# A hybrid SSM / gated-recurrence / expert-lookup layer: two buffers instead of three and another formula in the gated recurrence

## The reference, cut to what matters

```python
def rglru_scan(x, h0, lam, w_r, b_r, w_i, b_i):
    xb = x.reshape(x.shape[0], x.shape[1], LRU_HEADS, LRU_BLOCK)
    r = sigmoid(einsum('blhi,hij->blhj', xb, w_r).reshape(x.shape) + b_r)
    i = sigmoid(einsum('blhi,hij->blhj', xb, w_i).reshape(x.shape) + b_i)
    log_a = -LRU_C * r * softplus(-lam)
    a = exp(log_a)
    bx = sqrt(-expm1(2.0 * log_a)) * (i * x)
    bx = bx.at[:, 0].add(a[:, 0] * h0)
    _, h = lax.associative_scan(linear_combine, (a, bx), axis=1)
    return h, h[:, -1]
```

## Time and profile before

| | |
|---|---|
| median of 3 executions | 2747.85 us (2744.62 to 2749.66) |
| the profiled execution, its own time | 2744.62 us |
| its span, first to last instruction | 2742.8 us |
| PE busy | 2283.4 us (83%) |
| DVE busy | 1532.9 us (56%) |
| POOL busy | 1096.0 us (40%) |
| ACT busy | 422.4 us (15%) |
| mean granted TensorE clock | 0.946 |

### The profile page before, as it was taken

The page is one execution under the profiler, slowest core; times in us unless marked ns, Lnnn a source line. Parts: engine busy times, 40 slices in busy tenths (PEclk is TensorE's granted clock), DMA queues, the critical chain, the costliest instruction groups (busy, mean ns, idle before and its releaser), DMA issues.

```text
span 2742.8 us, 20845 instructions
## 1 busy us (share of the span) xinstructions
PE 2283.4 (83%) x7608; PEld 1320.0 (48%) x7608; DVE 1532.9 (56%) x2435; ACT 422.4 (15%) x788; POOL 1096.0 (40%) x905
## 2 busy tenths in 40 slices
PE   5989999899988996979996888777777777777777
PEld 2344447666766776868783344222222222222223
DVE  4424701999999992112275554556665566656441
ACT  3015600122222121000100111110111111111101
POOL 3000004366656661010045544555555555455541
PEclk9999999988888886999998999999999999999999
DMA  9931127666656653565489999999999999999995
GB/s 266 325 103 61 65 95 171 220 203 204 197 188 190 191 181 119 167 225 193 123 329 410 416 403 421 422 421 422 421 421 421 422 421 422 422 421 422 421 418 206
DMA packets 315206, 793.50 MB, mean 289 GB/s; under 512 B 25736, under 2 KB 243088, under 8 KB 247264
## 3 DMA queue, kind: packets, MB, share of 16 engines
q0 software_dynamic: 81600, 561.36, 50.4%
q1 hardware_dynamic: 223712, 225.55, 26.3%
q10 hardware_dynamic: 9792, 5.25, 0.8%
HBM read 778.40 MB, written 9.50 MB: 287 GB/s over the span
## 4 chain that ended last, share of the span: by engine, by line
DMA 32%; PE 15%; DVE 3%; POOL 3%; issue 2%; ACT 0%; DVEq 0%; ACTq 0%; POOLq 0%
DMA vb<-in_peer_v,eidx 28%; PE ps L1531 8%; PE ps L1478 4%; PE ps L1503 3%; DMA rows<-in_peer_u,eidx 2%; POOL vb L1246 1%; POOL rows L1246 1%; DMA mT<-in_peer_u,eidx 1%; POOL mT L1246 1%; DMA cut<-in_peer_sub_keys 1%; DVE rows L1438 0%; PE ps L1488 0%; PE ps L1513 0%; DVE mT L1438 0%; DVE f L1415 0%
## 5 line engine op out<-in xcount | busy, mean ns | idle before, releaser
L1531 PE MATMUL ps<-vb,diag 128*128 128x512 f32 x2048 | 946.1, 608 | 295.1 <-DMA vb<-in_peer_v,eidx 290.5
L1531 PEld LDWEIGHTS ps<-vb,diag 128*128 128x128 f32 x2048 | 374.4, 191 | 864.2 <-DMA vb<-in_peer_v,eidx 458.1
L1438 DVE CUSTOM_DVE_ANT_0 rows<-rows,f 128x2048 f32<-128x2048 f32 x170 | 387.5, 2291 | 334.9 <-DMA rows<-in_peer_u,eidx 334.6
L1246 POOL DMA_INDIRECT vb<-in_peer_v,eidx x256 | 366.7, 1433 | 485.0 <-PE ps L1531 465.6
L988 PE MATMUL ps<-nT,w_ring 128*128 128x256 f32 (+1 forms) x1792 | 540.2, 465 | 2.3 <-issue 1.7
L988 PEld LDWEIGHTS ps<-nT,w_ring 128*128 128x128 f32 x1792 | 363.0, 204 | 187.8 <-issue 144.8
L1438 DVE CUSTOM_DVE_ANT_0 mT<-mT,f 128x2048 f32<-128x2048 f32 x86 | 196.3, 2291 | 175.5 <-DMA mT<-in_peer_u,eidx 175.4
L1246 POOL DMA_INDIRECT rows<-in_peer_u,eidx x170 | 214.1, 1260 | 95.9 <-issue 48.1
L905 DVE SCALAR_TENSOR_TENSOR zu<-w_ring,scol,zu 128x256 f32<-128x256 f32 x448 | 208.0, 528 | 2.3
L1322 ACT ACTIVATE diag<-ident,wgt 128x128 f32<-128x128 f32 x256 | 94.1, 397 | 656.6 <-PE ps L1531 651.4
L1246 POOL DMA_INDIRECT mT<-in_peer_u,eidx x86 | 107.0, 1244 | 218.0 <-DVE eidx L1408 163.5
(11 more groups left out here) (325 smaller groups left out, 2066.3 us busy)
## 6 DMA issues: line engine op xcount, KB each, us to landing
w_ring<-in_w_ada SPq DMA_DIRECT2D x96, 1024.0 KB, 9.8
w_ring<-in_w_in SPq DMA_DIRECT2D x56, 1024.0 KB, 5.3
w_ring<-in_w_out SPq DMA_DIRECT2D x16, 1024.0 KB, 5.8
w_ring<-in_peer_w_query SPq DMA_DIRECT2D x16, 1024.0 KB, 11.6
w_ring<-in_w_proj_a SPq DMA_DIRECT2D x8, 1024.0 KB, 5.9
w_ring<-in_w_proj_b SPq DMA_DIRECT2D x8, 1024.0 KB, 5.9
gates_dram<-gst POOLq DMA_DIRECT2D x16, 256.0 KB, 6.3
big<-big SPq DMA_DIRECT2D x128, 32.0 KB, 5.4
```

Source lines behind the costliest of these rows:

```text
L1246: pool.indirect_dma_start(ring[m % n], None, table, bass.IndirectOffsetOnAxis(ap=eidx[:, i % 3, j:j + 1], axis=0))\
L1438: v.tensor_tensor_reduce(ub[m % n_u], ub[m % n_u], f[:, i // HEADS], 1.0, 0.0, ALU.mult, ALU.add, hd[:, i % 2, j:j + 1]).then_inc(u_used, 1)
L1531: last = pe.matmul(ps[:, 4 * tile + c, :], diag[:, m % NDIAG], vb[m % NV][:, c * 512:(c + 1) * 512], start=(r == 0), stop=(r == HEADS * K ...
```

## The change

The three tiles get two buffers instead of three, `gates(k)` waits for `lru_done` at k-1 from k = 2 on, and `q_of` computes the root's argument as 2t/(1+t) instead of (1+a^2)t.

```diff
-        rt = take(6 * 512).rearrange("p (b d n) -> p b d n", b=3, d=2)
-        ig = take(6 * 512).rearrange("p (b d n) -> p b d n", b=3, d=2)
-        ag = take(6 * 512).rearrange("p (b d n) -> p b d n", b=3, d=2)
+        rt = take(4 * 512).rearrange("p (b d n) -> p b d n", b=2, d=2)
+        ig = take(4 * 512).rearrange("p (b d n) -> p b d n", b=2, d=2)
+        ag = take(4 * 512).rearrange("p (b d n) -> p b d n", b=2, d=2)
...
             def gates(k):
 
-                b = k % 3
-                if k >= 3:
-                    act.wait_ge(lru_done, k - 2)
+                b = k % 2
+                if k >= 2:
+                    act.wait_ge(lru_done, k - 1)
...
-                    act.activation(rt[:, k % 3, d, :], rt[:, k % 3, d, :], ACT.Sqrt).then_inc(sq_done, 1)
+                    act.activation(rt[:, k % 2, d, :], rt[:, k % 2, d, :], ACT.Sqrt).then_inc(sq_done, 1)
...
             def q_of(k):
 
                 v.wait_ge(et_done, 4 * k + 4)
-                b = k % 3
-                step(tt(ltmp, ag[:, b], ag[:, b], ALU.mult))
-                stt(rt[:, b], ltmp, 1.0, rt[:, b], ALU.add, ALU.mult).then_inc(q_ready, 1)
+                b = k % 2
+                step(tsc(ltmp, rt[:, b], 1.0, None, ALU.add))
+                step(v.reciprocal(ltmp, ltmp))
+                stt(rt[:, b], rt[:, b], 2.0, ltmp, ALU.mult, ALU.mult).then_inc(q_ready, 1)
                 v.wait_ge(q_ready, k + 1)
 
             def scans(k):
-                b = k % 3
+                b = k % 2
```

## The result

The changed kernel takes 2794.61 us (median of 4 executions, 2794.18 to 2798.1) against 2746.82 us before (4 executions): 47.8 us more, a ratio of 1.0171 with a 95% interval of 1.0157 to 1.0185. The forecast was 2797 us, in a range from 2789 to 2808 us. Three more executions of the changed kernel are on record, at 2790.72, 2792.57 and 2793.56 us; the median of all seven is 2794.18 us. The profiled execution of the changed kernel is none of the four: its span of 2788.0 us is 4.4 us shorter than the shortest of theirs (2792.4 us), and 45.2 us longer than that of the profile before.

A forecast was written before the change was run, and what follows sets the result against it. The prediction took PE alone to bound the phase, with two buffers closing a longer ring through DVE and ACT. 47.67 us of lateness plus 2.0 us for PE's clock, 49.7 us, on 2747.85 us gave 2797 us, range 2789 to 2808 us.

The forecast's parts named there:

- PE as the bound of the phase: In the phase of the change PE alone sets the pace, 17.16 to 17.17 us a period, without idle time.
- The new formula: In q_of on DVE: add, reciprocal and product take 8.57 us, 6.05 us more; DVE's iteration becomes 18.10 us.
- The ring: Copy, convolution, q_of, scans, sigmoids, exponentials, tanh, roots, next copy in a row: 27.92 us; block 7 gates 47.67 us late.
- The first wait: PE waits for block 2's sigmoids ahead of block 3's gate products, starting at 259.98 instead of 255.32, 4.66 us late.
- The clock: PE restarts slower after each new wait; only the last, at block 7's gates, counts: 2.0 us, from 0 to 3.4.
- The hidden parts: Behind block 7's gates, the copy of accumulation 9 and DVE's last three scans stay covered and add nothing.
- The sum: Whole kernel: 47.67 + 2.0 = 49.7 us more than the median of 2747.85 us, forecast 2797 us.
- a reciprocal of eight cycles: Rival in q_of: reciprocal takes eight cycles an element, 8.7 us, giving +10.7 us and 2808 us; chance 5%.
- a cheap one: Rival in q_of: long reciprocal costs 1.22 us like its neighbours, ring 22.59 us, time 2771 us; chance 3%.
- a PE that stays slow: Rival: PE doesn't get back to 2.4 GHz between waits, its period becomes 34.3 us, some 2825 us; chance 3%.
- two buffers are enough: Rival: scans(i-3) is over when ACT asks at the first sigmoid, so no change, 2748 us; chance 2%.

The follow-up runs named there:

- the first experiment: Kernel before with its three buffers and waits, only q_of changed to the new formula with the reciprocal: 2747.74 us, ratio 1.0003.
- the fourth experiment: Changed kernel with one more reciprocal of the same length in each q_of, its result going to an unread tile: 2835.58 us, ratio to before 1.0316.
- the first three experiments: Kernel before with new formula, 2747.74 us; changed kernel with old formula, 2763.65 us; changed kernel with DVE order scans, q_of, conv, 2746.83 us.
- the third experiment: Changed kernel with DVE's order in an iteration turned round to scans, q_of, conv, same instructions: 2746.83 us, ratio 1.0001 to before.

## Why the prediction was right

- **PE as the bound of the phase.** Right, and shown from the other side by the first experiment: DVE work that makes PE wait for nothing is free here.
- **The new formula.** 8.57 us foreseen; the add 0.694 (0.70), the reciprocal 6.553 (6.55), DVE's work 18.10 us (18.10). The slope over 4, 16 and 64 elements held at 1024, which is 16 times the longest row. The Trainium skill ("VectorE: DVE Perf Modes", First, the fixed hardware budget) gives the divide a repeat count of 8; read as eight cycles an element, an estimate of 8.53 us, this is not what the reciprocal takes. For the add, the estimate of 0.69 us by its table (The perf-mode tier table) agrees with the measured 694 ns.
- **The ring.** 27.92 us foreseen, 27.68 measured. The terms that were off: DVE's signal to ACT took 0.04 us (256.92 to 256.96) and not 0.10, the way from copy to convolution 0.88 and not 0.91, and from the sigmoid to the next copy it took 8.66 us, not 8.76 + 0.05: the next copy starts at 265.62, before the second square root's end at 265.72. The first wait came out as foreseen, 259.53 - 237.71 = 21.82 us from the gates of block 2 to those of block 3 (4.66 us late). The four periods behind it were 0.24 us shorter each, about 1 us in all: the gates of block 7 came 132.52 us after those of block 2 instead of 85.83, **46.69 us** late where 47.67 were foreseen.
- **The clock.** 2.0 us foreseen at the last restart, 5.29 - 3.60 = 1.69 us measured. The granted clock was 0.85 over a period of the ring, where it had been 1.00 before. For the four waits ahead of the last it made no difference, since PE's slower work only shortened its waits: 7.92 us instead of the 10.75 in the prediction. That number was a delay per period, and the prediction gave it out for idle time where it says what the profile after would show; the idle rows have it less the clock's loss, which is about 2 us each time.
- **The hidden parts.** The copy of accumulation 9 and DVE's last scans did not show in the changed kernel; the first of them had 4.8 us in hand, and in the fourth experiment it became a wait.
- **The sum.** 46.69 + 1.69 = 48.4 us at the end of the phase, 47.8 us by the medians (49.7 foreseen). In the profiles the delay is 47.9 us at the start of the next columns (375.36 - 327.42; this profile was 0.45 us ahead at the gates of block 2), and 45.91 us at line 1121 (1122.47, against 1076.56 in the earlier trace rows), so some 2 us come back in the stages between. The granted clock is 0.85 in both there. These stages are not equally long from profile to profile: from PE's first products with `ones` (line 1110 before, 1111 after) to that line it is 571.6 us before, 569.8 us after, and 573.2 to 576.4 us in the first three experiments, whose changes don't touch them. So the 2 us need no cause in the change, and they are within the ±4 us that the prediction gave to these stages. Of the 2.4 us between the 2797 us forecast and the result, about 1 us is the median before, 2747.85 us then and 2746.82 us with the fourth execution.
- **The rivals.** Three of the four are refuted by the profile after: a reciprocal of eight cycles and a cheap one by 6553 ns, a PE that stays slow by the 13.90 us of the columns behind each wait, the same as before. That two buffers are enough is refuted by the wait of 16.86 us in this order of DVE's work; the third experiment shows that it is true in another order. The prediction took the order as given and did not see how little separates the two.

## What to carry to other kernels

One buffer less costs nothing or much, depending on whether the consumer's release stands, in its engine's order, behind something that waits for the producer in the same iteration; then the two engines take turns and every microsecond of either counts. Draw that ring from the program order before counting work, and if it closes, try the order first: releasing the buffer at the head of the iteration gave back all 48 us with the same instructions. That was over eight blocks; DVE stayed the slower engine by about 1 us a block. A busy share says little in both directions: an engine filled to its limit for some 90 us cost nothing, and no engine was full where 48 us were lost.

## What the runs showed of the hardware

The reciprocal on DVE takes 6553 ns for 128x1024 float32 and 553 ns for 128x64, 6.25 ns for each further element. That is over five times the 1225 ns of a pass with two tensors of 128x1024; a one-tensor add with a constant takes 694 ns.

In the three kernels of this study in which PE waits ahead of the gate products, the gate products were slow after each of the waits from 3.24 to 14.99 us and not after 1.38 or 2.52 us (3.67 us instead of 3.60). The loss did not grow with the wait: 2.91 us after 3.24 us of idle time (6.51 us), 1.69 us after 8.47 us (5.29 us), 1.87 us after 14.99 us (5.47 us). What sets its size was not tested.
